# Transposing x in pairs of 64 tokens on both halves of TensorE's rows, splitting it in half blocks, and cutting small products to their used parts

## The reference

```python
for i in range(2):                                   # first_block
    m = neighborhood_attention(...) if i == 0 else diff_attention(...)   # of rms_norm(x, g0)
    x = x + rms_norm(m, g1)
    x = x + rms_norm(conv_glu_ffn(rms_norm(x, g2), ...), g3)             # 1024 -> 2 x 2816 -> 1024
    x = x + sigmoid(rms_norm(x, g4) @ ple_w_gate) * (p[i] @ ple_w_proj)
# second_block
x = x + 0.5 * swiglu(rms_norm(x, ln_ffn1), w1_gate, w1_up, w1_down)
u = rms_norm(x, ln_mix) @ w_in                        # split into an HGRN2 part and a latent-attention part
x = x + concat(hgrn2(u), latent_attention(u)) @ w_out
x = x + 0.5 * swiglu(rms_norm(x, ln_ffn2), w2_gate, w2_up, w2_down)
x = x + sigmoid(rms_norm(x, ln_ple) @ w_ple_gate) * (p_2 @ w_ple_proj)
return rms_norm(x, ln_final)
```

## Time and profile before

| | |
|---|---|
| median of 3 runs | 1193.83 us (1193.21 to 1194.4) |
| the profiled execution | 1193.42 us |
| its span, first to last instruction | 1191.5 us |
| mean granted TensorE clock | 0.999 |
| PE busy | 1178.3 us (99%) |
| DVE busy | 931.6 us (78%) |
| ACT busy | 665.5 us (56%) |
| POOL busy | 140.2 us (12%) |

### The profile page before, as it was taken

The page is one execution under the profiler, slowest core; times in us unless marked ns, Lnnn a source line. Parts: engine busy times, 40 slices in busy tenths (PEclk is TensorE's granted clock), DMA queues, the critical chain, the costliest instruction groups (busy, mean ns, idle before and its releaser), DMA issues.

```text
span 1191.5 us, 17767 instructions
## 1 busy us (share of the span) xinstructions
PE 1178.3 (99%) x6915; PEld 1027.0 (86%) x6915; DVE 931.6 (78%) x1270; ACT 665.5 (56%) x1059; POOL 140.2 (12%) x265
## 2 busy tenths in 40 slices
PE   8999999999999999999999999999999999999997
PEld 7998988888889989888888988888898888888886
DVE  6867898898777689989888898766776778766765
ACT  6756644444867786544446745444586664444445
POOL 5300600000310011000003100000206410000002
PEclk9999999999999999999999999999999999999999
DMA  9748376655544455665555566556455147566540
GB/s 291 228 158 269 121 245 209 206 183 178 181 154 143 132 164 191 212 211 179 186 169 181 184 227 192 187 185 203 136 191 177 43 161 229 174 198 203 186 142 36
DMA packets 151671, 215.83 MB, mean 181 GB/s; under 512 B 7002, under 2 KB 116956, under 8 KB 151588
## 3 DMA queue, kind: packets, MB, share of 16 engines
q1 hardware_dynamic: 148124, 207.46, 52.8%
q0 software_dynamic: 1760, 3.94, 1.3%
q10 hardware_dynamic: 1704, 3.28, 0.9%
HBM read 213.60 MB, written 1.06 MB: 180 GB/s over the span
## 4 chain that ended last, share of the span: by engine, by line
PE 94%; DVE 2%; ACT 2%; POOL 1%; DMA 1%; issue 0%; SPq 0%; POOLq 0%; ACTq 0%; DVEq 0%
PE work L2507 25%; PE work L2510 13%; PE acc L2083 10%; PE acc L2084 10%; PE acc L2085 10%; PE work L2083 5%; PE work L2084 5%; PE work L2085 5%; PE work L2105 1%; PE work L2496 1%; PE work L2484 1%; PE work L2498 1%; DVE w_lo L1359 1%; PE acc L2140 1%; PE acc L2285 1%; PE work L2319 1%
## 5 line engine op out<-in xcount | busy, mean ns | idle before, releaser
L1359 DVE TENSOR_TENSOR w_lo<-raw,w_hi 128x2048 fp32r<-128x2048 f32 (+1 forms) x192 | 436.0, 2277 | 52.8 <-ACT w_hi L752 52.8
L752 ACT ACTIVATE w_hi<-raw 128x2048 fp32r<-128x2048 f32 (+1 forms) x192 | 363.7, 1899 | 71.3 <-PE work L2510 59.3
L2507 PE MATMUL work<-hT_both,w_hi 128*128 128x512 f32 x1280 | 318.8, 391 | 0.0
L2507 PEld LDWEIGHTS work<-hT_both,w_hi 128*128 128x128 f32 x1280 | 234.8, 188 | 45.2
L2510 PEld LDWEIGHTS work<-hT_both,w_lo 128*128 128x128 f32 x1280 | 174.6, 190 | 12.5
L2510 PE MATMUL work<-hT_both,w_lo 128*128 128x256 f32 x1280 | 178.5, 282 | 0.0
L2083 PE MATMUL acc<-w_hi,aux_hi 128*128 128x512 f32 x400 | 158.1, 395 | 0.0
L2084 PE MATMUL acc<-w_lo,aux_hi 128*128 128x512 f32 x400 | 156.7, 392 | 0.0
L2085 PE MATMUL acc<-w_hi,aux_lo 128*128 128x512 f32 x400 | 155.9, 390 | 0.0
L1133 ACT ACTIVATE aux_hi<-Z 128x256 fp32r<-128x256 f32 x88 | 37.0, 420 | 195.3 <-DVE Z L1781 107.4
L1752 DVE TENSOR_REDUCE Z<-work 128x256 f32<-128x512 f32 x88 | 60.6, 689 | 89.3 <-PE work L2510 87.6
(11 more groups left out here) (286 smaller groups left out, 1736.7 us busy)
## 6 DMA issues: line engine op xcount, KB each, us to landing
raw<-in_ffn_w_in SPq DMA_DIRECT2D x44, 1024.0 KB, 5.2
raw<-in_ffn_w_out SPq DMA_DIRECT2D x22, 1024.0 KB, 5.1
raw<-in_w_gate SPq DMA_DIRECT2D x22, 1024.0 KB, 5.4
raw<-in_w_up SPq DMA_DIRECT2D x22, 1024.0 KB, 5.3
raw<-in_w_down SPq DMA_DIRECT2D x22, 1024.0 KB, 5.0
raw<-in_da_w_qkv SPq DMA_DIRECT2D x12, 1024.0 KB, 5.3
raw<-in_na_w_qkv SPq DMA_DIRECT2D x10, 1024.0 KB, 8.1
raw<-in_ple_w_gate SPq DMA_DIRECT2D x8, 1024.0 KB, 5.2
```

The source lines that it names most:

```text
L752: act.activation(w_hi[:, n % RING, 0:size], raw[:, n % RAW, 0:size], ACT.Copy).then_inc(hi_done, 1)
L1359: dve.tensor_tensor(w_lo[:, n % RING, 0:size], raw[:, n % RAW, 0:size], w_hi[:, n % RING, 0:size].bitcast(F32), ALU.subtract).then_inc(lo_ ...
L2507: pe.matmul(b.rearrange("p (e s) -> p e s", e=2), v[0][:, k, cols(c % 2)], hT_both[:, k, :, :], start=k == 0, stop=False)
```

## The change

It has four parts. (1) Each transpose of 128 tokens becomes two of 64 tokens, one on rows 0 to 63 of the array and one on rows 64 to 127, whose results go to different banks: bank r holds the tokens of half r, for all 8 blocks. For the phases that transpose x outside ple, PE waits for both halves of the features of x before the first transpose. (2) Each split step covers the 64 tokens of one half of a block, 16 steps a tile; the counters go from 8 to 16, with the same distance of two steps between ACT and DVE, and ACT's first steps wait for all transposes of the tile. (3) In levels 1, 2 and 3 of the mixer, one product of 128 stationary by 64 moving columns becomes 2, 4 and 4 products with 32, 16 and 24 stationary and 32, 16 and 16 moving columns. (4) At the joint from phase 2 to 3, DVE's `add_gated(2, 2)` goes ahead of `normed(3, 0)`, and the splits, gates and squares are put in another order.

```diff
-        stage(f"n{ph}.{t}", 2 if PHASES[ph] == "ple" else 0, (0, 1) * 4)
+        stage(f"n{ph}.{t}", 2 if PHASES[ph] == "ple" else 0, (0, 1) * 8)
...
         def turned_block(ph, t, step):
-            half = acc[:, 2 * t + step % 2, :] if (ph, t) in ACC_TURN else bank(G[f"n{ph}.{t}"] + step % 2)
-            return half[:, step // 2 * P:(step // 2 + 1) * P]
+            k, r = split_order(ph)[step // 2], step % 2
+            half = acc[:, 2 * t + r, :] if (ph, t) in ACC_TURN else bank(G[f"n{ph}.{t}"] + r)
+            return half[:, k * 64:(k + 1) * 64]
+
+        def block_half(v, ph, t, step):
+            c = t * P + 64 * (step % 2)
+            return v[:, split_order(ph)[step // 2], c:c + 64]
 
         def split_done(eng, ph, t, k):
-            eng.wait_ge(part_ready, H[f"n{ph}.{t}"] - 8 + split_order(ph).index(k) + 1)
+            eng.wait_ge(part_ready, H[f"n{ph}.{t}"] - 16 + 2 * split_order(ph).index(k) + 2)
...
# ACT
-                    for i in steps:
+                    for i in range(2 * steps[0], 2 * steps[-1] + 2):
                         if i >= 2:
-                            act.wait_ge(part_ready, H[f"n{ph}.{t}"] - 8 + i - 1)
+                            act.wait_ge(part_ready, H[f"n{ph}.{t}"] - 16 + i - 1)
                         elif (ph, t) in ACC_TURN:
-                            act.wait_ge(turn_full, 2 * ACC_TURN.index((ph, t)) + i + 1)
+                            act.wait_ge(turn_full, 2 * ACC_TURN.index((ph, t)) + 2)
                         else:
                             full(act, G[f"n{ph}.{t}"] + i)
-                        k = split_order(ph)[i]
-                        split(hT_hi[:, k, t * P:(t + 1) * P], turned_block(ph, t, i), gains_of(ph, k))
+                        split(block_half(hT_hi, ph, t, i), turned_block(ph, t, i), gains_of(ph, split_order(ph)[i // 2]))
...
                     gates(2, 2)
                     gates(2, 3)
-                    tile_parts(3, 0, range(2))
                     pre(3, 1, (0,))
-                    tile_parts(3, 0, range(2, 4))
-                    pre(3, 1, (1,))
+                    tile_parts(3, 0, range(4))
                     gates(2, 4)
                     tile_parts(3, 0, range(4, 6))
+                    pre(3, 1, (1,))
+                    tile_parts(3, 0, range(6, 8))
                     pre(3, 1, (2,))
-                    tile_parts(3, 0, range(6, 8))
...
# DVE
-                    for i in steps:
-                        k, tile = split_order(ph)[i], slice(t * P, (t + 1) * P)
-                        split(hT_lo[:, k, tile], turned_block(ph, t, i), hT_hi[:, k, tile],
-                              H[f"n{ph}.{t}"] - 8 + i + 1, gains_of(ph, k))
+                    for i in range(2 * steps[0], 2 * steps[-1] + 2):
+                        split(block_half(hT_lo, ph, t, i), turned_block(ph, t, i), block_half(hT_hi, ph, t, i),
+                              H[f"n{ph}.{t}"] - 16 + i + 1, gains_of(ph, split_order(ph)[i // 2]))
...
                     add_gated(2, 1)
                     feed(b + 6)
+                    add_gated(2, 2)
                     normed(3, 0)
-                    add_gated(2, 2)
+                    tile_parts(3, 0, range(4))
                     add_gated(2, 3)
-                    tile_parts(3, 0, range(4))
+                    tile_parts(3, 0, range(4, 6))
                     add_gated(2, 4)
-                    tile_parts(3, 0, range(4, 8))
+                    tile_parts(3, 0, range(6, 8))
...
# PE, turn_x, ple
-                        ins = pe.transpose(b[k % 2][:, cols(k // 2)], x[:, t, cols(k)], ident[:, :])
-                        if k >= KT - 2:
-                            ins.then_inc(bank_full[(G[f"n{ph}.{t}"] + k % 2) % WORK], 1)
+                        for r in range(2):
+                            some = cols(r, 64)
+                            ins = pe.transpose(b[r][:, cols(k, 64)], x[some, t, cols(k)], ident[some, some])
+                            if k == KT - 1:
+                                ins.then_inc(bank_full[(G[f"n{ph}.{t}"] + r) % WORK], 1)
...
# PE, turn_x, the others
-                        whole = PHASES[ph - 1] == "ple" and t == 1
-                        if whole:
+                        if PHASES[ph - 1] == "ple" and t == 1:
                             pe.wait_ge(x_quarter, ple_index(ph - 1) + 1)
-                        pe.wait_ge(x_ready, 4 * (ph - 1) + 2 * t + (2 if whole else q + 1))
+                        pe.wait_ge(x_ready, 4 * (ph - 1) + 2 * t + 2)
...
-                    b = acc[:, 2 * t + q, :]
-                    for i in range(4):
-                        ins = pe.transpose(b[:, cols(i)], src[:, t, cols(4 * q + i)], ident[:, :])
+                    for k in range(4 * q, 4 * q + 4):
+                        for r in range(2):
+                            some = cols(r, 64)
+                            ins = pe.transpose(acc[:, 2 * t + r, cols(k, 64)], src[some, t, cols(k)], ident[some, some])
                     ins.then_inc(turn_full, 1)
...
# PE, level
-                                if 0 < i < QUAD:
+                                if 0 < i < 4:
+                                    m = LEVELS[i]
+                                    wide = max(2 * m, 32)
+                                    for b in range(P // wide):
+                                        c = t * P + b * wide
+                                        late = q[:, 2 * j + h, c:c + wide].rearrange("p (b e r) -> p b e r", e=2, r=m)
+                                        to = d[b * wide:(b + 1) * wide - m, (2 * h + t) * 64 + b * wide // 2:
+                                               (2 * h + t) * 64 + (b + 1) * wide // 2]
+                                        ins = pe.matmul(to.rearrange("p (b r) -> p b r", r=m),
+                                                        k[:, 2 * j + h, c:c + wide - m], late[:, :, 1, :],
+                                                        start=True, stop=True)
+                                elif i == 4:
```

## The result

The changed kernel takes 1227.03 us (median of 4 runs, 1226.16 to 1227.42), the kernel before 1193.59 us in the same series. The ratio is 1.0279 with a 95% interval of 1.0267 to 1.0291: slower by 33.4 us. The forecast was 1219 with a range of 1200 to 1231; the result lies in that range, and 1 us above the forecast's own 1211 to 1226.

A forecast was written before the change was run, and what follows sets the result against it. The prediction took PE, busy 99% of the span, as the bound. Splits +28.9, transposes -1.5 and small products -1.9 gave +25.5 on 1193.4, hence 1219 us; range 1200 to 1231, the forecast's own 1211 to 1226.

The forecast's parts named there:

- The price of a half step: Splits on ACT and DVE: 64 columns take 310 and 278 ns, so one block every 0.66 us instead of 0.39.
- That PE cannot hide it: Split chain works 43 us longer over 160 blocks; PE, with hardly any idle time, sees 28.9 us of it.
- cheap half steps: Rival on the splits: a step's fixed part is small, most waits vanish, 1190 us, down to 1181; chance 0.09.
- half hidden: Rival on the phase boundaries: later slack takes up half of the 28.9 us, giving 1204.5 us; chance 0.17.
- transposes that don't overlap: Rival on the paired transposes: the halves run one after the other, +6 instead of -1.5, 1226 us; chance 0.13.
- small products bound by issue: Rival on mixer levels 1 to 3: +4.5 instead of -1.9 us, giving 1225 us; chance 0.06.
- The sum over the boundaries: Delays PE sees from slower splits, worked out boundary by boundary over phases 0 to 9: +28.9 us.
- those of phases 3 and 6: Boundary terms for late splits and the additions around them at the starts of phases 3 and 6: +3.1 us each.
- phase 8: Boundary term: tile 1's splits begin 1.0 later behind DVE's weight conversion, blocks come slower than PE uses them: +2.7 us.
- Transposes: Paired 64-row transposes on PE: 0.45 us spared a tile, 0.37 lost to mode changes, -1.5 us in all.
- Small products: Mixer levels 1 to 3 on PE, 5.4 us before: 0.85, 1.3 and 1.3 after, so -1.9 us.
- The joint: Phase 2 to 3: the moved add fills 1.15 us of DVE idle time and spares tile 0 about 1.0, within +3.1.

The follow-up runs named there:

- Half splits alone: The kernel before with only the splits changed to 16 steps of 64 columns a tile, on its 128-token transposes: 1231.95 us, ratio 1.0320.
- the ple phases as before: The changed kernel with phases 2, 5 and 9 put back to whole-block splits and 128-token transposes: 1217.09 us, ratio 1.0194.
- the filled one: The changed kernel plus unneeded identity products in PE's idle time ahead of the first transposes of phases 3 and 6: 1227.15 us, ratio 1.0281.
- with pairs: The changed kernel with the old joint order and old levels 1 to 3, keeping paired transposes and half-block splits: 1230.12 us, ratio 1.0303.
- the joint undone: The changed kernel with the old order at the joint of phases 2 and 3: 1229.72 us, ratio 1.0301.

## Why the prediction was right, and where it was off

**The price of a half step: right.** Forecast 0.31 and 0.28 us, measured 0.312 and 0.283; the period 0.66, measured 0.66. The line through two sizes of the same instruction was worth more than a figure from elsewhere. The table in the Trainium skill, "VectorE: DVE Perf Modes", section on the TRN2 errata, gave an estimate of 0.46 us a block; that is under the 0.48 from which the prediction let the waits vanish, so a faster kernel would have been forecast from it.

**That PE cannot hide it: right.** Half splits alone cost 38.3 us; 43 had been reckoned on the chain of ACT and DVE. The rivals "cheap half steps" and "half hidden" are out. The two rivals whose number came nearest, transposes that don't overlap (1226) and small products bound by issue (1225), are out by their rows: the 33 us come from neither.

**The sum over the boundaries: 28.9 was too small.** The loss is 33.4 us where 25.5 was forecast in all, and this term is the reason. The terms that were mis-sized are those of phases 3 and 6, "+3.1" each: I counted what the splits of those phases do themselves, and that part came out to 0.3 us (3.1 and 3.4 with the ple phases as before), in phase 3 perhaps by luck, since it rests on 1.0 spared by the joint's order that was not measured there. I had treated tile 1's splits of a ple phase as harmless, since PE uses those blocks at 0.68 us; I didn't follow ACT's queue behind them, where the feed, the table load and the gates stand that the next phase's x needs. That is 2.3 us in each of the two, of which the slow clock may have up to 0.3 in phase 3. The other miss is phase 8, 4.1 instead of 2.7. There the clock was low in the profiled execution of the changed kernel and not in that of the filled one, over the same stretch (changed kernel, then the filled one):

```profile
1000.00:1012.00 12.00, 10.28 (x76) 9.29 (x76) 8.87 (x26) 8.47 (x31) 4.65 (x7) 0.86 0.47 153
```

```profile
1000.00:1012.00 12.00, 10.05 (x77) 8.46 (x76) 9.56 (x30) 9.36 (x36) 4.64 (x7) 1.00 0.37 119
```

PE's step at that boundary is 0.8 us smaller in the second (3.3). Of either step 0.25 is the wait that the small products leave behind, at the end of phase 7. Without it the step is 3.6 to 3.8 in the four executions whose clock fell there (the changed kernel, half splits alone, with pairs, the ple phases as before), and 3.0 in the two whose clock did not (filled, the joint undone). So some 0.6 to 0.8 of the 1.4 goes with the clock, and 0.3 stays open.

**Transposes: the overlap right, the sign by luck.** The pairs do overlap: their two records start 3 to 4 ns apart, and pairs follow one another at 0.062 us (forecast 0.057). But the sum took 0.11 us for a transpose before, and 17 us for 160, where 0.80 us for eight is 0.10 and 16; with 0.10 only 0.34 a tile would have been spared against 0.37 for the changes of mode, and the term would have come out at about +0.5. (Its bounds are rounded alike: 20 times 0.45 is 9.0, not 8.6, and 20 times 0.37 is 7.4, not 6.) PE's rows give about -0.05 a tile, -1 us in all, because the changes cost less than 0.37. The 1.8 us in the medians is not the pairs' alone.

**Small products: the size on PE right, the gain not.** -1.9 was forecast, PE's difference is -1.7, but the medians show -0.7 on the kernel before and -0.4 in the changed one (1230.12 to 1229.72). Levels 2 and 3 are shorter than forecast, and the waits in level 1 and behind level 3 take part of it back. On the kernel before, the spans show 1.5 us of gain; the medians show less, since more time lies around the span. In the changed kernel, -0.4 is within the spread of the runs (1229.01 to 1230.94).

**The joint: undervalued.** I had it as part of phase 3's +3.1, with about 1.0 spared. It spares 2.7 us in the changed kernel, where the splits are what PE waits for, though part of it may be the place at which the clock falls: 8.0 to 7.0 in phase 3 where that place is the same. On the kernel before it is some 0.7 at best.

Step by step, the medians go from 1193.7 before by +38.3 (half splits), -1.8 (pairs), -0.4 (small products) and -2.7 (joint) to 1227.0. Each step is the difference of two neighbouring kernels, so the sum is no test; only the first and the last are clear of the spread.

## What to carry to other kernels

Cutting the instructions of a chain in half pays only where their duration goes with their size. Here some 300 ns of 350 stayed, and two engines that hand steps to one another through two banks delivered two steps per round trip: two blocks in 0.78 us before, two halves of one in 0.66 after. When such a chain gets slower, don't stop at its own consumer: follow each engine's queue behind it to the next thing that PE will wait for, a feed, a gate, an addition. And before a slow clock after a stall is called a cost, ask what PE does with the time that it gets back, and look where the clock falls instead.

## What the runs showed of the hardware that was not expected

The granted clock fell to 0.50 after a wait of PE of 2.61 us (0.57 over 686 to 690, with products of 256 columns 0.21 us apart) and after a wait of 1.45 us (0.50 over 349 to 352). With products in the idle time it stayed at 1.00 in those places and fell to 0.50 at 355.3 and at 700.0 instead, and the kernel was no faster.

Two transposes of 64 tokens on the two halves of the rows started 3 to 4 ns apart, a pair every 0.062 us; the change into this mode put 0.08 us between the product ahead and the first pair.

Plain fp32 products of 16 stationary by 16 moving columns, on four strips of columns, ran 64 in 0.70 us, about 0.01 us each.
